# Trading five sum products of both router norms for GpSimd additions, and handing over the sum over experts in two parts

## What is computed

```python
def rms_norm(x, g):
    xf = x.astype(jnp.float32)
    y = xf * lax.rsqrt(jnp.mean(xf * xf, axis=-1, keepdims=True) + NORM_EPS)
    return (y * g.astype(jnp.float32)).astype(x.dtype)
...
for i in range(DEPTH):
    ...                                    # token mixer, y_p and y_s updated
    y_p = y_p + g2_p[:, None, :] * moe(modulate(y_p, norm_ffn[i], sh2_p, sc2_p), *mw)
    y_s = y_s + g2_s[:, None, :] * moe(modulate(y_s, norm_ffn[i], sh2_s, sc2_s), *mw)
```

## Time and profile before

| | before |
|---|---|
| median of 3 runs | 1283.17 us (1282.88 to 1284.16) |
| profiled execution | 1284.74 us, of which the span of the trace is 1282.9 us |
| PE busy | 1255.7 us (98%) |
| DVE busy | 444.4 us (35%) |
| ACT busy | 328.3 us (26%) |
| POOL busy | 72.5 us (6%) |
| granted TensorE clock, mean | 0.996 |
| HBM | 387 GB/s over the span |

### The profile page before, as it was taken

How to read it: one execution, slowest core, us unless ns; L and a number is a source line. 1 busy time by engine, 2 the same in 40 slices (tenths; PEclk the granted TensorE clock), 3 DMA queues, 4 the chain that set the end, 5 groups by cost and what they waited for, 6 DMA issues and landing times.

```text
span 1282.9 us, 18946 instructions
## 1 busy us (share of the span) xinstructions
PE 1255.7 (98%) x6950; PEld 695.9 (54%) x6950; DVE 444.4 (35%) x1508; ACT 328.3 (26%) x736; POOL 72.5 (6%) x119
## 2 busy tenths in 40 slices
PE   7999999999999999999999899999999999999998
PEld 5776775544454445444454477554455445544544
DVE  3596272222222222222235727322222222222223
ACT  2486331221122112211122523222122211221211
POOL 0395000000000000000010020000000000000000
PEclk8999999999999999999999999999999999999999
DMA  9988999999999999999997787899999999999994
GB/s 328 383 329 360 406 417 383 415 420 419 421 420 420 421 421 420 420 420 420 419 407 322 167 366 263 288 404 418 419 420 420 420 420 421 420 421 421 419 419 193
DMA packets 90760, 497.44 MB, mean 388 GB/s; under 512 B 11273, under 2 KB 20145, under 8 KB 38480
## 3 DMA queue, kind: packets, MB, share of 16 engines
q1 hardware_dynamic: 90128, 496.48, 96.1%
q10 hardware_dynamic: 576, 0.22, 0.1%
HBM read 493.26 MB, written 3.41 MB: 387 GB/s over the span
## 4 chain that ended last, share of the span: by engine, by line
PE 93%; DVE 3%; ACT 2%; DMA 1%; issue 1%; ACTq 0%; POOL 0%; DVEq 0%
PE ps L1105 35%; PE ps L1139 18%; PE ps L1150 10%; PE ps L1076 7%; PE ps L781 4%; PE ps L706 4%; PE ps L834 3%; PE ps L1012 2%; PE ps L659 2%; PE ps L1125 1%; PE ps L1060 1%; PE ps L1117 1%; DMA W<-in_norm_ffn_dram 1%; PE ps L719 1%; PE ps L679 1%
## 5 line engine op out<-in xcount | busy, mean ns | idle before, releaser
L1105 PE MATMUL ps<-ring,xg 128*64 128x512 f32 x1344 | 296.4, 593 | 0.3
L1105 PEld LDWEIGHTS ps<-ring,xg 128*64 128x64 f32 x1344 | 101.5, 137 | 189.6 <-issue 175.2
L1105 PE MATMUL ps<-S,xg 128*64 128x512 f32 x704 | 154.8, 592 | 0.0
L1139 PE MATMUL ps<-ring,W 128*64 128x512 f32 x672 | 153.5, 598 | 0.0
L2186 DVE TENSOR_TENSOR ypart<-ps,ypart 128x512 fp32r<-128x512 f32 x128 | 88.5, 691 | 179.7 <-ACT ypart L1641 179.7
L2175 DVE SCALAR_TENSOR_TENSOR vec<-silu_h,W,ps 128x256 f32<-128x256 f32 x64 | 30.7, 480 | 332.2 <-ACT silu_h L1635 332.2
L1150 PEld LDWEIGHTS ps<-comb,ypart 128*128 128x128 f32 x1024 | 126.5, 191 | 18.6 <-issue 18.6
L1150 PE MATMUL ps<-comb,ypart 128*128 128x256 f32 x1024 | 135.3, 285 | 0.0
L1635 ACT ACTIVATE silu_h<-ps 128x256 f32<-128x256 f32 x64 | 24.7, 385 | 406.6 <-PE ps L1105 406.6
L1630 ACT ACTIVATE xg<-ps 128x384 f32<-128x384 f32 x176 | 83.3, 492 | 167.9 <-PE ps L1076 167.9
L1641 ACT ACTIVATE ypart<-ps 128x512 fp32r<-128x512 f32 x128 | 76.5, 597 | 184.6 <-PE ps L1139 184.6
(11 more groups left out here) (288 smaller groups left out, 1101.7 us busy)
## 6 DMA issues: line engine op xcount, KB each, us to landing
ring<-in_exp_w_down_dram SPq DMA_DIRECT2D x86, 1024.0 KB, 17.5
ring<-in_exp_w_gate_dram SPq DMA_DIRECT2D x78, 1024.0 KB, 15.9
ring<-in_exp_w_up_dram SPq DMA_DIRECT2D x78, 1024.0 KB, 18.3
S<-in_exp_w_down_dram SPq DMA_DIRECT2D x44, 1024.0 KB, 17.6
S<-in_exp_w_gate_dram SPq DMA_DIRECT2D x40, 1024.0 KB, 17.4
S<-in_exp_w_up_dram SPq DMA_DIRECT2D x40, 1024.0 KB, 19.0
ring<-in_ada_w_dram SPq DMA_DIRECT2D x24, 1024.0 KB, 20.3
S<-in_ada_w_dram SPq DMA_DIRECT2D x16, 1024.0 KB, 15.2
```

Source lines behind the costliest of these rows:

```text
L1105: mm = pe.matmul(PGU[64 * b:64 * b + 64, :].rearrange("p (h f) -> p h f", h=2), xg[:, places[k][m], 64 * b:64 * b + 64], gate_up_of(w[b])[ ...
L1139: mm = pe.matmul(bank[64 * b:64 * b + 64, :], hidT[:, j, 64 * b:64 * b + 64], down_of(w[b])[:, j, n * 512:(n + 1) * 512], start=(j == 0), ...
```

## The change

Both router norms: GpSimd adds the squares 1 to 5 to square 0, one after another (`add_squares`), each addition waiting for its square and for the addition before it. TensorE multiplies the sum and the squares 6 and 7 with the ones (`added_squares`), three products where there were eight. Their place in TensorE's list is that of the eight. In GpSimd's list `add_squares(0)` stands ahead of the updates between the layers, and `add_squares(1)` behind the scaling of the router weights.

Sum over experts: `acc_done` rises twice in a mixture, once after the steps q = 0, 1 (the chunks 0, 1, 4, 5) and once after 2, 3. VectorE starts on the first rise, ScalarE on the second. Between the layers VectorE's order becomes 0, 1, 4, 5, 2, 3, its squares 4, 5, 3, and TensorE sums in the order 0, 1, 2, 4, 5, 3, 6, 7.

```diff
-DVE_SQUARES = (3, 4, 5)
+DVE_SQUARES = (4, 5, 3)
-LATENT_ORDER = (0, 1, 2, 3, 4, 5, 6, 7)
+LATENT_ORDER = (0, 1, 2, 4, 5, 3, 6, 7)
+UPDATE_ORDER = ((0, 1, 4, 5, 2, 3), (0, 1, 2, 3, 4, 5))
+SUMMED = 6
...
+            def added_squares(l, bank):
+
+                pe.wait_ge(cv_added, additions(2, addends(2)) + (SUMMED - 1) * (l + 1))
+                pe.matmul(bank[:, 0:TT], ones, sq[:, 0, :], start=True, stop=False)
+                for k in range(SUMMED, KC):
+                    pe.wait_ge(sq_ready, KC * (2 * l + 2) + k + 1 + N_LATENT_ACT * l)
+                    mm = pe.matmul(bank[:, 0:TT], ones, sq[:, k, :], start=False, stop=(k == KC - 1))
+                mm.then_inc(ss_ready, 1)
...
-                sum_squares(3 if l == 0 else 5, 7 if l == 0 else 1)
+                added_squares(l, ps[7] if l == 0 else ps[1])
...
-                    return mm
+                        if q % 2 == 1:
+                            mm.then_inc(acc_done, 1)
...
-                spill_combine().then_inc(acc_done, 1)
+                spill_combine()
...
+            def add_squares(l):
+
+                for k in range(1, SUMMED):
+                    pool.wait_ge(sq_ready, KC * (2 * l + 2) + k + 1 + N_LATENT_ACT * l)
+                    if k > 1:
+                        pool.wait_ge(cv_added, additions(2, addends(2)) + (SUMMED - 1) * l + k - 1)
+                    pool.tensor_tensor(sq[:, 0, :], sq[:, 0, :], sq[:, k, :], ALU.add).then_inc(cv_added, 1)
+
+            add_squares(0)
...
+            add_squares(1)
...
-                dve.wait_ge(acc_done, l + 1)
+                dve.wait_ge(acc_done, 2 * l + 1)
                 dve.wait_ge(y_moved, 32 * (l + 1))
+                for n, k in enumerate(UPDATE_ORDER[l]):
+                    if k == 2:
+                        dve.wait_ge(acc_done, 2 * l + 2)
+                    if l == 0:
+                        updated_y(0, k, 1).then_inc(y_latent, 1)
+                    else:
+                        updated_y(l, k, 0)
+                        updated_y(l, k, 1).then_inc(y_ready, 1)
```

More of the change, by code:

```diff
@@ L677, in sum_squares @@
                     k = SUM_ORDER[i] if n == 2 else i
-                    pe.wait_ge(sq_ready, KC * (n - 1) + i + 1 + (N_LATENT_ACT if n == 5 else 0))
+                    pe.wait_ge(sq_ready, KC * (n - 1) + i + 1)
                     mm = pe.matmul(ps[bank][:, 0:TT], ones, sq[:, k, :], start=(i == 0), stop=(i == KC - 1))
@@ L1326, in gate_y @@
             def gate_y(l):
-                act.wait_ge(acc_done, l + 1)
+                act.wait_ge(acc_done, 2 * l + 2)
                 for k in range(KC - 2, KC):
@@ L1341, in latent_norm_first @@
                 load_table(ACT.Sqrt)
-                act.wait_ge(acc_done, 1)
+                act.wait_ge(acc_done, 2)
                 for k in (KC - 2, KC - 1):
@@ L1346, in latent_norm_first @@
                     if k not in DVE_SQUARES:
-                        act.wait_ge(y_latent, KC + k + 1)
+                        act.wait_ge(y_latent, KC + UPDATE_ORDER[0].index(k) + 1)
                         act.activation(sq[:, k, T:TT], yT[:, k, T:TT], ACT.Square).then_inc(sq_ready, 1)
@@ L2299, in _ @@
                     dve.wait_ge(moe_done, l + 1)
-                dve.wait_ge(acc_done, l + 1)
+                dve.wait_ge(acc_done, 2 * l + 1)
                 dve.wait_ge(y_moved, 32 * (l + 1))
+                for n, k in enumerate(UPDATE_ORDER[l]):
[6 more added lines that the diff above has]
+                        updated_y(l, k, 1).then_inc(y_ready, 1)
                 if l == 0:
-                    for k in range(KC - 2):
-                        updated_y(0, k, 1).then_inc(y_latent, 1)
                     for k in DVE_SQUARES:
-                        dve.wait_ge(y_latent, KC + k + 1)
+                        dve.wait_ge(y_latent, KC + UPDATE_ORDER[0].index(k) + 1)
                         dve.tensor_tensor(sq[:, k, T:TT], yT[:, k, T:TT], yT[:, k, T:TT], ALU.mult
@@ L2311, in _ @@
                         updated_y(0, k, 0).then_inc(y_ready, 1)
-                else:
-                    for k in range(KC - 2):
-                        updated_y(l, k, 0)
-                        updated_y(l, k, 1).then_inc(y_ready, 1)
             dve.wait_ge(y_tr, 4)
```

## The result

The changed kernel's median is 1287.18 us (1283.6 to 1288.71, 11 runs), that of the kernel before beside it 1283.61 us (1282.88 to 1284.98, 11 runs). The ratio is 1.0026, 95% interval 1.0019 to 1.0034: 3.6 us slower, outside the forecast range of 1281.1 to 1285.0. Run again beside the experiments it was 1285.93 us against 1283.23, ratio 1.0018 (1.0009 to 1.0026), 2.7 us slower. The profiled execution took 1286.8 us, with a span of 1285.0 us against 1282.9.

What follows compares the result with a forecast made beforehand. TensorE was taken to bound the kernel, the expert loop's length being fixed; +1.2 + 0.9 - 0.3 - 1.25 - 0.8 = -0.25 us on 1283.17 gave 1282.9 us, range 1281.1 to 1285.0.

Steps and rivals of the forecast that it cites:

- Layer 0's additions, +1.2: Layer 0's router norm: GpSimd's five additions, 0.86 us apart, end the sum of squares 1.2 us later.
- The clock in layer 0, "I take 0.9": Layer 0's norm: TensorE's 3.3 us hole lets its clock fall, slowing the sum's three products by 0.9 us.
- as long as the low clock ends as soon as it did at 658.24: Layer 0: condition under which slow conditioning products cost nothing more, as VectorE paces the router's products.
- Rival 3: Layer 0's low clock outlasts the conditioning products and delays the router's: total +3.85, 1287.0 us; chance 0.05.
- Handover, -0.3: Between the layers: VectorE's earlier start saves TensorE's wait for its first square, about 0.3 us, bounds 0 and 0.5.
- Layer 1, -1.25: Layer 1's router norm: three products instead of eight start the router's products and all that follows 1.25 us earlier.
- nearly all of the 1.25 us passes: Layer 1: a 0.8 us wait for the shared expert's weights merely replaces the 0.78 us wait for VectorE's selection.
- Rival 2: Layer 1: late shared-expert weights shrink the gain to 0.4 or less, 1283.8 us; chance 0.18 together with rival 5.
- The hole of TensorE is under 1 us, shorter than the one that left the clock alone: Layer 1's norm: TensorE's new hole is too short to lower the clock, so no clock cost was counted.
- End, -0.8: Kernel's end: VectorE starts its twelve last updates on the first rise, gaining 0.8 us, bounds 0.5 and 0.8.
- the third chunk is due when the second rise has long come: Kernel's end: VectorE's updates, started early, would not have to wait for the second half of the products.
- Rival 5: Branches before VectorE's updates hide the split handover: end 0.5, handover nothing, 1283.5 us; chance 0.18 together with rival 2.

Runs made afterwards that it cites:

- e2: The kernel before with only layer 0's additions on GpSimd; 1287.04 us, +3.18 us to the kernel before, ratio 1.0020.
- e1: The kernel before with only layer 1's additions on GpSimd; 1284.01 us, +0.15 us to the kernel before, ratio 1.0002.
- e3: The kernel before with only the sum over experts handed over in two parts; 1282.49 us, -1.37 us to the kernel before, ratio 0.9992.
- e6b: The changed kernel with ten two-column products added at the start of TensorE's list; 1284.41 us, +0.92 us to the kernel before.
- e7b: The kernel before with the handover in two parts, layer 1's additions and earlier shared-expert up and down transfers; 1280.62 us, -2.87 us to before.
- e5: The changed kernel with six filling products in layer 1 ahead of the wait for the shared expert's weights; 1284.05 us, +0.82 us to the kernel before.
- e4: The changed kernel with layer 1's shared-expert up and down transfers issued earlier; 1285.98 us, +2.12 us to the kernel before.
- e10: e7b with three of layer 0's squares summed on GpSimd (two additions) and TensorE taking the other five; 1280.60 us, -2.63 us to the kernel before.
- e8b: The kernel before with layer 0's additions alone and 14 filling products in TensorE's hole; 1284.70 us, +1.21 us to the kernel before.
- e11: The changed kernel with 64 tiny products (256 instructions) at the start of TensorE's list; 1285.95 us, +2.72 us to the kernel before.
- e12: The changed kernel run again, unchanged; 1285.93 us, +2.70 us to the kernel before, ratio 1.0018.

## Why the prediction was wrong

It gave "same" 0.88 and "slower" 0.05. The sum was -0.25 us; measured was +3.6 and +2.7. In medians the parts add up: +3.18 (e2) + 0.15 (e1) - 1.37 (e3) + 1.2 (the stall that only the combination has) = 3.2. Against the terms of the sum, layer 0 is 1.1 worse (+2.1 was forecast), layer 1 is 1.4 worse (-1.25), the stall is 1.2 that no term had, and handover and end together are 0.3 better (-1.1).

- **Layer 0's additions, +1.2: right.** They are 0.87 us apart, the root is 1.23 us later with the clock at 1.00, and the run that filled the hole has +1.21.
- **The clock in layer 0, "I take 0.9": the fall was right, the size too small.** The low clock began before the three products and covered them in five of the six falls; they then cost 1.4 more (2.60 - 1.23), above even the 1.3 that was the upper bound. In the median filling the hole gives back 2.0. The other 0.6 between the root's 2.60 and the median's 3.18 weren't isolated; that profile has its second low-clock stretch in layer 1. The premise "as long as the low clock ends as soon as it did at 658.24" (3.4 us) did not hold either: the low clock lasted 6.8 us in those five, as the first fall in the earlier trace rows did, and 3.4 in e6b. But that did no harm. Rival 3, the low clock that outlasts the conditioning products, ended at 1287.0 us, near the measured time, and had 0.05; its mechanism did not come, so the closeness is luck. The 7.67 us from the root to the transposes did not move at the low clock, because VectorE's chunks cover the products.
- **Handover, -0.3: right**, 0.25. In the profiles the stretch shrank by 1.36, of which 1.1 is the fall of the clock in before's own profile. One of the four profiles with the old handover has that fall and none of the ten with the new one, too few to credit the change with it.
- **Layer 1, -1.25: the step that failed is "nearly all of the 1.25 us passes".** The root came 1.09 us earlier. But the transfer took 11.1 us in the changed kernel and in e1, where I carried over 10.5, and the shared expert did not start earlier at all. What stays is the old wait, 0.78: 0.73 measured in e1's profile, above the lower bound of 0.4. Rival 2 had this late transfer, at a price that proved too high.
- **Layer 1, the clock: a term put at nothing.** "The hole of TensorE is under 1 us, shorter than the one that left the clock alone" rested on one hole. The clock fell between 779 and 792 in seven of the ten profiles with layer 1's additions, in one of the four without. It cost 2.2 to 2.7 us where it covered the eleven products (22 records) ahead of the selection (18.62 and 19.12 us from squares to selection, 16.41 without); where it ended 1.7 us into them (e7b) they took 5.61 us in place of 4.86, 0.75 more. That this is what brings e1's median from -0.73 to +0.15 is the reading that fits: its fastest execution, at 1281.96 us, has a mean granted clock of 0.999 and its slowest, at 1286.75 us, 0.992. With one profile for each kernel it isn't shown that the additions make the falls more frequent.
- **End, -0.8: the mechanism right (0.85 in e3), the sum wrong.** In the combination 0.37 is lost (9.78 against 9.41). The step "the third chunk is due when the second rise has long come" held, but the sum took it that the transposes then follow the updates. Nothing in it, and no rival, had the stall of 1.36 to 1.80 us that hangs on the length of TensorE's list.
- **Rival 5** (branches hide the split) didn't come: the updates start right behind the subtraction.

What stays open: what makes the clock fall in layer 1. It isn't only the hole ahead of the shared expert, since it fell with that hole filled (e5) and with the transfer early (e4, e7b, e10). Fewer sum products right before it, and so a less busy TensorE, are my reading, which no run isolates and which e2's fall, with all eight products in place, does not support.

## What to carry to other kernels

Taking products away from an engine that clocks down when idle is only a gain if the replacement is ready when that engine comes for it: add up the helper's whole chain (five dependent additions, 4.2 us here) against the engine's own time for the same work (3.7 us), and give the helper only the share that hides, here two additions of five (which moved the root in the profile, but not yet the median). Price a fall of the clock by the products that would run under it, with the longest low stretch seen as the bound, and don't put it at nothing on the word of a single hole; one execution with or without a fall says little. If a small edit moves something that it doesn't touch, look for a hole whose named releaser was long done, compare the instruction queues, and shift the list by a few instructions before you judge the edit.

## What the runs showed of the hardware

- **A stall that depends on the length of TensorE's list.** 1.36 to 1.80 us between two products of one loop; ten two-column products (40 instructions) elsewhere in the list took it away, 64 (256 instructions) brought it back. The profile puts it down to VectorE, whose update for the next product was done 1.4 us before.
- **The granted clock differs from execution to execution of one program.** The changed kernel's eleven runs have means from 0.991 to 0.996 and times from 1288.71 to 1283.6 us, in that order; the kernel with every hole filled has 0.996 to 1.000 and a spread of 1.5 us. The Trainium skill ("TensorE: Matmul & The Clock Gate", "Part 1: The HAM clock gate") says that the number of slow products at a kernel's start varies from run to run; here the falls in the middle vary from run to run too.
- **The same transfer, 10.4 to 11.7 us.** 1024 KB of the shared expert's weights, third in a row of three issued behind the projection: 10.4 to 10.5 us to landing before, in e3, e6b and e8b; 11.0 to 11.1 in both profiles of the changed kernel, in e1, e5 and e11; 11.7 in e2. So it is not layer 1's additions that make it late: e2 has none, and e6b, which is the changed kernel with a longer list, has the short time. How soon the next expert's transfers are issued behind it doesn't decide it either: 2.53 us after it in e6b (10.4) and in e12 (11.1). What does is open.
